# Weights of an encoder trunk handed over as contiguous 256x512 blocks

## The reference

```python
for layer in range(DEPTH):                      # 2
    h = rms_norm(x, norm_w[layer])
    if layer % 2 == 0:
        z = h @ w_in_ab                         # 4096 x 13312
        qa, ka, va, qb, kb, vb, gate = split_cols(z, ...)
        oa = global_gqa(axial_rope(rms_norm(qa)), axial_rope(rms_norm(ka)), va)
        ob = neighbourhood_attention(qb, kb, vb, rpb)
        x = x + (concatenate([oa, ob]) * silu(gate)) @ w_out_ab      # 4096 x 4096
    else:
        z = h @ w_in_c                          # 4096 x 10240
        oc = window_gqa_sink(qc, kc, vc, sink)
        x = x + (oc * silu(gate)) @ w_out_c     # 4096 x 4096
return rms_norm(x, final_norm_w)
```

## Time and profile before

| | |
|---|---|
| median of 3 runs | 2860.01 us (2857.12 to 2866.35) |
| profiled execution | 2860.33 us |
| its span, first to last instruction | 2858.5 us |
| mean granted TensorE clock | 0.993 |
| TensorE busy | 2817.0 us (99%) |
| VectorE busy | 1692.7 us (59%) |
| ScalarE busy | 1339.4 us (47%) |
| queue 1 (SP): packets, MB, share of 16 engines | 341280, 593.52, 66.5% |
| queue 10 (ACT): packets, MB, share of 16 engines | 13968, 41.95, 4.2% |

### The profile page before, as it was taken

How to read it: one execution, slowest core, us unless ns; L and a number is a source line. 1 busy time by engine, 2 the same in 40 slices (tenths; PEclk the granted TensorE clock), 3 DMA queues, 4 the chain that set the end, 5 groups by cost and what they waited for, 6 DMA issues and landing times.

```text
span 2858.5 us, 37755 instructions
## 1 busy us (share of the span) xinstructions
PE 2817.0 (99%) x12681; PEld 2337.6 (82%) x12681; DVE 1692.7 (59%) x2102; ACT 1339.4 (47%) x1653; POOL 16.4 (1%) x14
## 2 busy tenths in 40 slices
PE   9999999999999999999999999999999999999998
PEld 7778778788888888888888888888888888878886
DVE  7656666555646556466655555666654666665554
ACT  5445444444544444444444445555544555443333
POOL 0000000000000000000000000000000000000000
PEclk9999999999999999999999999999999999999999
DMA  9666666777767767678777767677766777786665
GB/s 334 192 198 217 209 217 205 224 228 211 240 193 243 222 201 240 208 239 266 239 227 233 232 214 216 220 224 230 225 214 202 224 222 222 235 286 199 192 194 180
DMA packets 355379, 637.17 MB, mean 223 GB/s; under 512 B 25136, under 2 KB 78896, under 8 KB 355248
## 3 DMA queue, kind: packets, MB, share of 16 engines
q1 hardware_dynamic: 341280, 593.52, 66.5%
q10 hardware_dynamic: 13968, 41.95, 4.2%
HBM read 585.56 MB, written 49.81 MB: 222 GB/s over the span
## 4 chain that ended last, share of the span: by engine, by line
PE 89%; DMA 5%; DVE 4%; ACT 1%; issue 1%; SPq 1%; DVEq 0%; POOLq 0%; POOL 0%; ACTq 0%
PE proj L1061 29%; PE proj L1062 28%; PE proj L1063 28%; DMA landing<-group_turn 2%; DMA head_land<-head_turn 1%; DVE w_lo L725 1%; DMA group_turn<-q_stage 1%; PE sc_ps L1061 1%; PE o_ps L1061 1%; PE o_ps L1062 1%; PE o_ps L1063 1%; PE sc_ps L1063 1%; PE sc_ps L1062 1%; DMA head_turn<-head_stage 0%; ACT w_hi L600 0%
## 5 line engine op out<-in xcount | busy, mean ns | idle before, releaser
L725 DVE TENSOR_TENSOR w_lo<-raw,w_hi 128x1024 fp32r<-128x1024 f32 x990 | 1208.6, 1221 | 793.8 <-ACT w_hi L600 781.8
L600 ACT ACTIVATE w_hi<-raw 128x1024 fp32r<-128x1024 f32 x990 | 1049.9, 1060 | 1017.4 <-PE proj L1063 921.5
L1061 PE MATMUL proj<-w_hi,h_hi 128*128 128x512 f32 x2940 | 1149.9, 391 | 8.1 <-DVE w_lo L725 3.5
L1062 PE MATMUL proj<-w_lo,h_hi 128*128 128x512 f32 x2940 | 1148.2, 391 | 0.0
L1063 PE MATMUL proj<-w_hi,h_lo 128*128 128x512 f32 x2940 | 1147.7, 390 | 0.0
L1061 PEld LDWEIGHTS proj<-w_hi,h_hi 128*128 128x128 f32 x2940 | 554.8, 189 | 122.5 <-DVE w_lo L725 4.7
L1063 PEld LDWEIGHTS proj<-w_hi,h_lo 128*128 128x128 f32 x2940 | 554.1, 188 | 116.2
L1062 PEld LDWEIGHTS proj<-w_lo,h_hi 128*128 128x128 f32 x2940 | 554.9, 189 | 111.2
L1061 PE MATMUL proj<-w_hi,y_hi 128*128 128x512 f32 x1024 | 399.2, 390 | 0.0
L1062 PE MATMUL proj<-w_lo,y_hi 128*128 128x512 f32 x1024 | 399.1, 390 | 0.0
L1063 PE MATMUL proj<-w_hi,y_lo 128*128 128x512 f32 x1024 | 398.8, 389 | 0.0
(11 more groups left out here) (115 smaller groups left out, 1003.9 us busy)
## 6 DMA issues: line engine op xcount, KB each, us to landing
raw<-in_w_in_ab SPq DMA_DIRECT2D x415, 512.0 KB, 4.3
raw<-in_w_in_c SPq DMA_DIRECT2D x320, 512.0 KB, 4.6
raw<-in_w_out_ab SPq DMA_DIRECT2D x128, 512.0 KB, 4.6
raw<-in_w_out_c SPq DMA_DIRECT2D x128, 512.0 KB, 3.9
head_turn<-head_stage SPq DMA_DIRECT2D x256, 96.0 KB, 1.9
head_land<-head_turn ACTq DMA_DIRECT2D x64, 384.0 KB, 5.8
landing<-group_turn ACTq DMA_DIRECT2D x31, 512.0 KB, 6.5
group_turn<-q_stage SPq DMA_DIRECT2D x64, 128.0 KB, 3.0
```

What stands on the lines that cost most here:

```text
L600: nc.scalar.activation(w_hi[:, slot], raw[:, slot], ACT.Copy).then_inc(hi_ready, 1)
L725: nc.vector.tensor_tensor(w_lo[:, slot], raw[:, slot], w_hi[:, slot].bitcast(F32), ALU.subtract) \
L1061: nc.tensor.matmul(dst, hi, r_hi, start=start, stop=False)
L1062: nc.tensor.matmul(dst, hi, r_lo, start=False, stop=False)
```

## The change

The host hands each weight matrix over in another order: for each block of 256 rows and each group of 512 columns one contiguous piece, in which the two rows that a partition needs (p and 128 + p) lie side by side. The load of a block then reads, for each of 128 partitions, one run of 1024 numbers (4 KB) where it read two runs of 512 numbers (2 KB) that lay 128 rows apart. The pitch between one partition's run and the next is 4 KB; it was one row of the matrix (52 KB in w_in_ab, 40 KB in w_in_c, 16 KB in the two others). Tiles in SBUF, bytes, slots, waits and computation are the same.

```diff
@@ the load in SP's loop @@
-                    src = w[c * 2 * P:(c + 1) * 2 * P, bass.ds(col + step * p.i, GRP)]
+                    src = w[c, bass.ds(col // GRP + step // GRP * p.i, 1)]
                     if not (p.n0 == 0 and b == 0):
-                        sp.dma_start(raw[:, b % RING], src.rearrange("(j p) n -> p j n", p=P)) \
+                        sp.dma_start(raw[:, b % RING], src.rearrange("a p j n -> p (a j) n")) \
                             .then_inc(raw_loaded[b % RING], 16)
@@ the two half loads of the first block, on ScalarE's queue @@
             for j in range(2):
-                nc.scalar.dma_start(raw[:, 0, j], w_in_ab[j * P:(j + 1) * P, A_K:A_K + GRP]) \
+                nc.scalar.dma_start(raw[:, 0, j], w_in_ab[0, A_K // GRP, :, j]) \
                     .then_inc(half_loaded[j], 16)
@@ on the host @@
+def weight_layout(w):
+    return w.reshape(KC // 2, 2, P, w.shape[1] // GRP, GRP).transpose(0, 3, 2, 1, 4)
...
-        "w_in_ab": a["w_in_ab"][0],
-        "w_out_ab": a["w_out_ab"][0],
-        "w_in_c": a["w_in_c"][0],
-        "w_out_c": a["w_out_c"][0],
+        "w_in_ab": weight_layout(a["w_in_ab"][0]),
+        "w_out_ab": weight_layout(a["w_out_ab"][0]),
+        "w_in_c": weight_layout(a["w_in_c"][0]),
+        "w_out_c": weight_layout(a["w_out_c"][0]),
```

## The result

The changed kernel is slower. Median 2874.34 us of 18 runs (2864.15 to 2883.51) against 2859.33 us of 18 runs of the kernel before (2854.23 to 2866.35); the ratio is 1.0052, 95% interval 1.0041 to 1.0063. The forecast was 2856.5 us, with a range up to 2866. The profiled execution took 2875.36 us (span 2873.6), 15.1 us more span than before.

A forecast was written before the change was run, and what follows sets the result against it. The prediction took TensorE (99% busy) as the bound, with weight loads hidden except ahead of late transposes through DRAM. 51 loads x 0.074 us took 3.8 us off 2860.3, giving 2856.5 us, range 2848 to 2866.

The forecast's parts named there:

- What bounds the kernel: TensorE, busy 99%; steady-state weight loads are hidden, so only its waits for transposes through DRAM could be shortened.
- prediction's own sign of being wrong: TensorE's waits change by more than 9 us in either direction, or the 2.72 us of a block do.
- The gain of 0.074 us a load: Transfer of a 512 KB weight load in a backlog: 1.28 us in 4 KB runs against 1.35 in 2 KB runs.
- the estimate from the Trainium skill: Fixed overhead of about 3 cycles a packet: 131 against 134 cycles, 0.03 us a load, 1.5 us in all, time 2858.8.
- My pair of rows: Two backlog profile windows: 2 KB weight loads at 24.2 bytes/ns and engine, a 4 KB-run fetch at 25.6.
- The forecast's own sum: 51 loads ahead of late transposed tiles and heads, at 0.074 us each: 3.8 us off 2860.3, giving 2856.5; chance 0.58.
- rival A: Longer weight runs crowd a fetch sharing the engines: 2864.9 us, or 2868.7 without the 3.8 us gain; chance 0.15.
- 14 waits x 0.60: Rival A's cost: each late fetch's 8 runs an engine wait 75 ns more, 0.60 us a fetch, 8.4 us in all.
- The argument against A: No byte of a fetch moved until two of three loads ahead were through, so bytes ahead must be moved anyway.
- 2864.9 us: Rival A's time: 8.4 us more for late fetches, less the forecast's 3.8 us, if engines take one run per queue.
- Rival B: Weight loads in one contiguous piece also run faster outside a backlog: 2851.1 down to 2839, about 2849; chance 0.12.
- Rival C: Weight loads not moved in longer runs, or the gain goes where nobody waits: 2860 us; chance 0.15.

The follow-up runs named there:

- experiment 1: Changed kernel's contiguous 512 KB blocks, but each load again 256 runs of 2 KB: 2854.58 us, ratio 0.9990 to the kernel before.
- experiment 2: 4 KB runs as in the changed kernel, but partitions a whole double row apart, not contiguous: 2872.26 us, ratio 1.0048 to the kernel before.
- experiment 3: Changed kernel's contiguous blocks in four parts, a load being 512 runs of 1 KB: 2859.27 us, ratio 1.0005 to the kernel before.
- experiments 9 and 10: One weight load per head held by one block, in contiguous blocks: 4 KB runs (changed kernel) 2854.41 us, then 2 KB runs 2849.2 us.
- experiment 4: Kernel before, 2 KB weight runs; only a head's fetch cut into 256 runs of 1.5 KB instead of 128 of 3 KB: 2894.82 us, ratio 1.0121.

## Why the prediction was wrong

**What bounds the kernel.** Right as far as the runs tell: ScalarE's waits for weight loads stayed near 30 us in all (34 before, 27 after), and what moved the time is the fetches. 5.2 of the 15.1 us are busy time of TensorE and are not traced to them. By the prediction's own sign of being wrong (TensorE's waits change by more than 9 us) it was wrong: its idle time grew by 9.9 us.

**The gain of 0.074 us a load** was mis-sized. Over the whole execution queue 1 went from 19.5 to 593.52 MB / (0.648 x 16 x 2873.6 us) = 19.9 bytes/ns and engine, so a load takes 1.645 us of each engine in place of 1.679: 0.03 us. This is the size that the estimate from the Trainium skill ("DMA: Bandwidth & Descriptors", "Why small descriptors are slow") gave for the longer runs. But the agreement is partly luck: by the same working experiment 1, contiguous in 2 KB runs, has 1.653 us, and experiment 2, in 4 KB runs that are not contiguous, 1.670. In these single profiles most of the 0.03 us came with the contiguous block, and 0.01 us with the length. My pair of rows compared two windows of 0.5 and 3 us. Nor did the gain reach the end where it should: the waits for qT_lo are 15.8 us (10 times), not 12.4.

**The step that failed** is what longer weight runs cost a fetch. The forecast's own sum put it at nothing, on the ground that what is ahead of a fetch must be moved anyway; rival A counted it, but for "14 waits x 0.60" only. I let the slowdown act only where TensorE already waited, 5 heads and 9 turned tiles, and never asked what covers the other 59 of the 64 fetches of a head. They had little left. What the runs showed in its place: the median of a head's fetch rose by 0.7 us, ScalarE's waits for the 64 fetches from 224.4 to 275.1 us, 0.8 us a fetch, and TensorE's waits for headT_lo from 5 to 20, 10.5 us more; the time rose by 15.0 us where 3.8 off was forecast. The price of A is then not 14 x 0.6 but what 64 fetches lose beyond their cover; and the cover is no number of the list of waits, which knows only those who came late.

That the 0.60 us was nearly right is partly luck. It was worked out from one weight run for each run of the fetch; the packets have 305 weight runs before and 184 after beside 128 of the fetch, and its bytes took 0.51 us longer at the median.

**The argument against A**, that the fetch goes in the order of issue and whatever is ahead must be moved anyway, was read from one fetch of a turned tile, and for turned tiles it held (6.5 to 6.6 us). It does not hold for heads, of which there are twice as many. The two windows above show a fetch of a head sharing the engines with weights at 49 and 54%. The rule of the Trainium skill that I set against it ("DMA: Bandwidth & Descriptors", "Queues, rings and completion order": the engines go round the queues packet by packet) had only 0.15. I read its packet as one run, and 2864.9 us came from that reading; the page itself has about 9 to 17 descriptors in a packet. That the two queues share the engines, as the rule says, agrees with the windows above. How much an engine takes from a queue in one turn is not shown: the traces do not tell the engines apart, and experiment 3 speaks against one run in turn, since runs of 1 KB would then have made the fetches clearly faster than before.

**Rival B** (contiguity makes it faster) is worth about 0.1% by experiment 1 (0.9980 to 0.9999). **Rival C** is out: packets fell by exactly half of the weights' runs.

**Left open**: how the engines share out between the two queues, and with it why 1 KB runs are not faster than 2 KB; what the 5.2 us between experiments 9 and 10 are; and the 2.8 us of TensorE's busy time that the form of the record does not explain.

## What to carry to other kernels

In this kernel two DMA queues met on the same engines, and going from 2 to 4 KB runs on one of them slowed the small transfers of the other. Lengthening the runs of a transfer that nobody waits for can thus slow a small one that somebody does. Before such a change, count all the small transfers and ask for each how late it may come, not only for those that are late already. If they meet, try moving one issue by one block: here it was worth 0.6% with 4 KB runs (ratios 1.0052 to 0.9993), more than any form of the bulk transfer. Then look at every transfer behind the one that was moved: moved by two blocks, the load delayed the puts (1.9 to 3.9 us) and cost 1.2% against the kernel before.

## What the runs showed of the hardware that I had not expected

Time on the engines per byte hardly depends on the length of a run between 1 and 4 KB. Worked out from queue 1's share of each span, a load of 512 KB in a contiguous block takes 1.667 us of each engine in 1 KB runs (experiment 3: 65.9% of 2863.2 us), 1.653 in 2 KB runs (experiment 1: 65.5% of 2857.2) and 1.645 in 4 KB runs (the changed kernel: 64.8% of 2873.6); not contiguous it takes 1.679 in 2 KB runs (before) and 1.670 in 4 KB runs (experiment 2). Between the queues the length counts much more: halving the runs of the 384 KB fetch (experiment 4) raised its median from 5.8 to 6.8 us.

After a short wait for a head (1.0 us without a matmul, near 1112 us in the changed kernel) the granted clock stayed at the upper level; busy time of each engine, then PEclk, DMA share, GB/s:

```profile
1111.00:1116.50 5.50, 4.49 (x24) 3.52 (x23) 4.15 (x6) 4.09 (x5) 0.00 (x0) 1.00 0.32 95
```

After the wait of 3.36 us for a turned tile that ended at 313.1 us in the kernel before it was 0.65 on average over 4.9 us, and so it was after a wait of 1.79 us for a head that ended at 2101.1 us:

```profile
2101.10:2106.00 4.90, 4.88 (x17) 4.05 (x18) 3.67 (x5) 2.66 (x4) 0.00 (x0) 0.65 0.44 115
```

The prediction named such a fall only for the waits of some 3 us; the wait of 1.79 us was followed by one as well.
